# The 13 RMS norms of a two-block transformer kernel: squares taken from PSUM, sums on VectorE, root and reciprocal with tokens on partitions

## The reference, cut to what matters

```python
def rms_norm(x, w):
    xf = x.astype(jnp.float32)
    y = xf * lax.rsqrt(jnp.mean(xf * xf, axis=-1, keepdims=True) + EPS)
    return (y * w.astype(jnp.float32)).astype(x.dtype)
...
# first block, each layer (the ctx rows likewise in layer 0)
h_lat = rms_norm(x, norm_pre_mix[l]) * (1.0 + sc1) + sh1
x = x + g1 * rms_norm(y_lat, norm_post_mix[l])
h_lat = rms_norm(x, norm_pre_ffn[l]) * (1.0 + sc2) + sh2
x = x + g2 * rms_norm(conv_ffn(h_lat, ...), norm_post_ffn[l])
...
# second block, each layer, and at the end
x = x + token_mixing(x, mix_norm_g[l], ...)
h = rmsnorm(x, ffn_norm_g[l])
x = x + swiglu(h, ...)        # layer 0; a mixture of 8 experts in layer 1
return rmsnorm(x, final_norm_g)
```

## Time and profile before

| what | us |
|---|---|
| median of 3 runs | 3615.11 (3614.79 to 3618.42) |
| time of the profiled execution | 3617.53 |
| span of the profiled execution | 3615.8 |
| PE busy in it | 3414.6 |
| DVE busy | 793.5 |
| ACT busy | 670.2 |
| POOL busy | 129.4 |

### The profile page before, as it was taken

The page is one execution under the profiler, slowest core; times in us unless marked ns, Lnnn a source line. Parts: engine busy times, 40 slices in busy tenths (PEclk is TensorE's granted clock), DMA queues, the critical chain, the costliest instruction groups (busy, mean ns, idle before and its releaser), DMA issues.

```text
span 3615.8 us, 75672 instructions
## 1 busy us (share of the span) xinstructions
PE 3414.6 (94%) x32538; PEld 2801.5 (77%) x32539; DVE 793.5 (22%) x1762; ACT 670.2 (19%) x1444; POOL 129.4 (4%) x173
## 2 busy tenths in 40 slices
PE   7999689999989899999999999989999999999998
PEld 3456638884357688787788887779999999988898
DVE  1114626660111421113210023130000100011001
ACT  2224112220112431112210021201111111110011
POOL 0000010010000100010000010000000000000000
PEclk9999699999999999999999999989999999999999
DMA  6446011222223243343344433238999999954477
GB/s 247 183 164 225 11 47 70 93 70 72 78 82 103 90 151 130 115 146 110 116 140 144 158 128 105 100 111 320 358 350 370 372 354 352 370 188 154 136 267 272
DMA packets 94761, 637.59 MB, mean 176 GB/s; under 512 B 10784, under 2 KB 11824, under 8 KB 38592
## 3 DMA queue, kind: packets, MB, share of 16 engines
q1 hardware_dynamic: 92048, 627.58, 47.2%
q0 software_dynamic: 2608, 8.49, 0.7%
HBM read 634.98 MB, written 1.05 MB: 176 GB/s over the span
## 4 chain that ended last, share of the span: by engine, by line
PE 91%; DVE 4%; ACT 2%; DMA 2%; issue 1%; POOL 0%; SPq 0%; DVEq 0%; ACTq 0%
PE bank L504 23%; PE bank L924 20%; PE bank L594 18%; PE bank L545 7%; PE bank L614 5%; PE bank L516 4%; PE bank L881 2%; PE bank L468 2%; PE bank L478 1%; PE bank L650 1%; PE bank L939 1%; PE bank L632 1%; PE bank L639 1%; DVE RT L1437 1%; DVE Y L1454 1%
## 5 line engine op out<-in xcount | busy, mean ns | idle before, releaser
L504 PE MATMUL bank<-H,ring 128*128 128x256 f32 (+1 forms) x3040 | 774.1, 417 | 19.6 <-ACT H L1095 16.5
L504 PEld LDWEIGHTS bank<-H,ring 128*128 128x128 f32 x3040 | 581.2, 192 | 197.7 <-issue 127.2
L594 PE MATMUL bank<-PROJ,ring 128*64 128x96 f32 (+2 forms) x7776 | 668.0, 282 | 12.3 <-ACT SC L1136 9.6
L594 PEld LDWEIGHTS bank<-PROJ,ring 128*64 128x64 f32 (+1 forms) x7776 | 547.6, 147 | 131.3 <-issue 98.1
L924 PE MATMUL bank<-MIX,ring 128*64 128x96 f32 x12544 | 524.2, 247 | 10.8 <-issue 10.8
L924 PEld LDWEIGHTS bank<-MIX,ring 128*64 128x64 f32 x12544 | 522.4, 138 | 13.1 <-issue 12.9
L1821 DVE TENSOR_TENSOR PROJ<-SC,bank 128x96 f32 (+2 forms) x246 | 71.0, 288 | 626.1 <-ACT SC L1277 621.9
L924 PE MATMUL bank<-H,ring 128*128 128x256 f32 x896 | 193.7, 379 | 0.0
L924 PEld LDWEIGHTS bank<-H,ring 128*128 128x128 f32 x896 | 170.2, 190 | 23.4 <-issue 0.3
L614 PE MATMUL bank<-H,ring 128*128 128x256 f32 x768 | 178.6, 391 | 3.9 <-ACT PROJ L1158 3.7
L614 PEld LDWEIGHTS bank<-H,ring 128*128 128x128 f32 x768 | 148.5, 196 | 28.2 <-issue 7.4
(11 more groups left out here) (310 smaller groups left out, 2705.3 us busy)
## 6 DMA issues: line engine op xcount, KB each, us to landing
ring<-in_moe_up SPq DMA_DIRECT2D x224, 1024.0 KB, 6.0
ring<-in_moe_down SPq DMA_DIRECT2D x128, 896.0 KB, 6.0
ring<-in_up SPq DMA_DIRECT2D x44, 1024.0 KB, 4.8
ring<-in_mod_b SPq DMA_DIRECT2D x40, 1024.0 KB, 5.0
ring<-in_tproj SPq DMA_DIRECT2D x32, 1024.0 KB, 4.8
ring<-in_proj SPq DMA_DIRECT2D x26, 1024.0 KB, 4.8
ring<-in_gates SPq DMA_DIRECT2D x24, 1024.0 KB, 4.8
ring<-in_down SPq DMA_DIRECT2D x32, 704.0 KB, 4.1
```

Of the source, the lines that this page charges most:

```text
L504: mm = pe.matmul(B[(tile + t) % 4][:, 0:width], w[:, k, t * P:(t + 1) * P], src[:, k, 0:width], start=k == 0, stop=k == k_n - 1)
L594: mm = pe.matmul(B[bank][lo:lo + m, 0:width], w[:, k, lo:lo + m], src(s * half + k), start=s == 0 and k == 0, stop=s == 1 and k == half - 1)
```

## The change

- Post norms: ACT squares each tile from its PSUM bank into H and then copies it to Y with the factor AB as the copy's scale (`take_tile`). The tiles of an output projection are taken one by one, for which PE counts a new semaphore `half_unit` behind the first tile of each unit.
- DVE adds the squares of tiles 1 to 6 onto that of tile 0 (`sum_square`) for norms 0, 1, 3, 5, 7, 9, 10 and 11; PE then takes the means of two tiles (the sum, and tile 7). Norms 2, 4, 6, 8 and 12 keep a step for each of the 8 tiles.
- PE's means have the squared tile as weights and one column of constants as moving operand; tokens come out on partitions, in 4 columns of bank 7 (2 at width 256). ACT takes the root and DVE the reciprocal of these columns in `stat`, and PE spreads them into bank 4, which DVE's multiplies read.
- DVE multiplies a whole tile at once without the factor; in pre norms of the first block the factor is the scale of ACT's shift. DVE, not POOL, makes the residual adds.
- The square-root table of ACT is called up ahead of norms 0, 1, 3, 5, 7, 9, 10, 11 and 12 by a root of one column.

The diff, cut to its core:

```diff
+        HALF_OF = {"wout0": 0, "wout1": 4, "twout0": 8, "twout1": 12}
+        def tile_in(name, k):
+            if k % 2 == 0:
+                return S("half_unit"), HALF_OF[name] + k // 2 + 1
+            return unit_done, base[name] + k // 2 + 1
...
-            def norm(n, width):
-
-                for k in range(KT):
-                    pe.wait_ge(S(f"norm{n}_sq"), k + 1)
-                    mm = pe.matmul(B[4][:, 0:width], mean_d, H[:, k, 0:width], start=k == 0, stop=k == KT - 1)
-                mm.then_inc(S("norm_ms"), 1)
+            def norm(n, width, summed):
+
+                def means(k, first, last):
+                    for c in range(width // P):
+                        mm = pe.matmul(B[7][:, c:c + 1], H[:, k, c * P:(c + 1) * P], mean_d[:, 0:1], start=first and c == 0, stop=last,
+                                       skip_group_check=True)
+                    return mm
+
+                if summed:
+                    pe.wait_ge(S("norm_acc"), summed)
+                    means(0, True, False)
+                    pe.wait_ge(S(f"norm{n}_sq"), KT)
+                    means(KT - 1, False, True).then_inc(S("norm_ms"), 1)
+                else:
+                    for k in range(KT):
+                        pe.wait_ge(S(f"norm{n}_sq"), k + 1)
+                        mm = means(k, k == 0, k == KT - 1)
+                    mm.then_inc(S("norm_ms"), 1)
+                pe.wait_ge(S("norm_r"), n + 1)
+                for c in range(width // P):
+                    mm = pe.matmul(B[4][:, c * P:(c + 1) * P], stat[:, c:c + 1].to_broadcast([P, P]), ident, start=True, stop=True)
+                mm.then_inc(S("norm_b"), 1)
...
-                act.activation(RT[:, 0:width], B[4][:, 0:width], ACT.Sqrt, bias=eps).then_inc(S("norm_rt"), 1)
+                act.activation(stat[:, 0:width // P], B[7][:, 0:width // P], ACT.Sqrt, bias=eps).then_inc(S("norm_rt"), 1)
...
                 for k in range(KT):
+                    act.wait_ge(S(f"norm{n}_scaled"), k + 1)
                     for s in range(width // T):
-                        act.wait_ge(S(f"norm{n}_scaled"), k * (width // T) + s + 1)
                         part = H[:, k, s * T:(s + 1) * T]
-                        act.activation(part, part, ACT.Identity, bias=MOD[:, l, sh + k, s:s + 1]).then_inc(S(f"norm{n}_out"), 1)
+                        act.activation(part, part, ACT.Identity, bias=MOD[:, l, sh + k, s:s + 1], scale=AB[:, row, k, s:s + 1])\
+                           .then_inc(S(f"norm{n}_out"), 1)
...
+            def sqrt_table(src):
+                act.activation(qw[:, :], src, ACT.Sqrt)
+            def take_tile(n, k, bank, row, width):
+
+                act.activation(H[:, k, 0:width], bank[:, 0:width], ACT.Square).then_inc(S(f"norm{n}_sq"), 1)
+                for s in range(width // T):
+                    ins = act.activation(Y[:, k, s * T:(s + 1) * T], bank[:, s * T:(s + 1) * T], ACT.Copy, scale=AB[:, row, k, s:s + 1])
+                ins.then_inc(lin_free, 1)
...
+            def down_to_y(n, name, width):
+                sqrt_table(eps)
+                for k in range(KT):
+                    act.wait_ge(unit_done, base[name] + 2 * k + 2)
+                    take_tile(n, k, B[k % 2], 3, width)
...
+            def sum_square(n, k, width):
+
+                dve.wait_ge(S(f"norm{n}_sq"), k + 1)
+                ins = dve.tensor_tensor(H[:, 0, 0:width], H[:, 0, 0:width], H[:, k, 0:width], ALU.add)
+                if k < KT - 2:
+                    step(ins)
+                else:
+                    ins.then_inc(S("norm_acc"), 1)
+
             def recip_root(n, width):
                 dve.wait_ge(S("norm_rt"), n + 1)
-                step(dve.reciprocal(RT[:, 0:width], RT[:, 0:width]))
+                dve.reciprocal(stat[:, 0:width // P], stat[:, 0:width // P]).then_inc(S("norm_r"), 1)
+                dve.wait_ge(S("norm_b"), n + 1)
...
+                    dve.tensor_tensor(H[:, k, 0:width], X[:, k, 0:width], B[4][:, 0:width], ALU.mult).then_inc(S(f"norm{n}_scaled"), 1)
...
+            def residual(n, width):
+
+                for k in range(1, KT - 1):
+                    sum_square(n, k, width)
                 recip_root(n, width)
+                for k in range(KT + 1):
+                    if k < KT:
+                        dve.tensor_tensor(Y[:, k, 0:width], Y[:, k, 0:width], B[4][:, 0:width], ALU.mult).then_inc(S(f"norm{n}_scaled"), 1)
+                    if k > 0:
+                        dve.wait_ge(S(f"norm{n}_scaled"), k)
+                        dve.tensor_tensor(X[:, k - 1, 0:width], X[:, k - 1, 0:width], Y[:, k - 1, 0:width], ALU.add)\
+                           .then_inc(S(f"norm{n}_out"), 1)
...
-            residual(3, TC)
+            pool.wait_ge(S("norm_ms"), 4)
             for v in range(2, 2 * C_HEADS):
```

More of the change, by code:

```diff
@@ L493, in mod_step, with fm_unit @@
                     mod_turn(n - 1)
-            def fm_unit(u, tile, src, width, it=0, tiles_per_it=0, k_n=KT, ready=None, mod=None):
+            def fm_unit(u, tile, src, width, it=0, tiles_per_it=0, k_n=KT, ready=None, mod=None, half=False):
                 w = unit(u, it).rearrange("p (k n) -> p k n", n=2 * P)
@@ L505, in fm_unit @@
                                        start=k == 0, stop=k == k_n - 1)
+                    if t == 0 and half:
+                        mm.then_inc(S("half_unit"), 1)
                     if t == 0 and mod is not None:
@@ L521, in wout @@
                 for j in range(4):
-                    fm_unit(base[name] + j, tile_base[name] + 2 * j, src, width, ready=ready if j == 0 else None)
+                    fm_unit(base[name] + j, tile_base[name] + 2 * j, src, width, ready=ready if j == 0 else None, half=True)
             def pairs(name, width, ready):
@@ L1071, in _ @@
             moe()
-            norm(12, T)
+            norm(12, T, 0)
         @block.scalar
@@ L1439, in modulate @@
-            def modulate(n, row, width):
+                dve.reciprocal(stat[:, 0:width // P], stat[:, 0:width // P]).then_inc(S("norm_r"), 1)
+                dve.wait_ge(S("norm_b"), n + 1)
+            def modulate(n, width):
                 recip_root(n, width)
                 for k in range(KT):
-                    for s in range(width // T):
-                        cols = slice(s * T, (s + 1) * T)
-                        dve.scalar_tensor_tensor(out=H[:, k, cols], in0=X[:, k, cols], scalar=AB[:, row, k, s:s + 1],
-                                                 in1=RT[:, cols], op0=ALU.mult, op1=ALU.mult).then_inc(S(f"norm{n}_scaled"), 1)
@@ L1448, in gate @@
-            def gate(n, row, width):
-                recip_root(n, width)
-                for k in range(KT):
-                    for s in range(width // T):
-                        cols = slice(s * T, (s + 1) * T)
-                        dve.scalar_tensor_tensor(out=Y[:, k, cols], in0=Y[:, k, cols], scalar=AB[:, row, k, s:s + 1],
-                                                 in1=RT[:, cols], op0=ALU.mult, op1=ALU.mult).then_inc(S(f"norm{n}_scaled"), 1)
+                    dve.tensor_tensor(H[:, k, 0:width], X[:, k, 0:width], B[4][:, 0:width], ALU.mult).then_inc(S(f"norm{n}_scaled"), 1)
@@ L1863, in _ @@
             step(dve.tensor_copy(lmask[:, :], SC[:, 0:6 * 32]))
+            for k in range(1, KT - 1):
+                sum_square(0, k, TC)
             dve.wait_ge(S("consts_in"), 16)
@@ L1951, in _ @@
             step = Chain(pool, "pool_step")
-            def residual(n, width):
-                for k in range(KT):
-                    pool.wait_ge(S(f"norm{n}_scaled"), (k + 1) * (width // T))
-                    pool.tensor_tensor(X[:, k, 0:width], X[:, k, 0:width], Y[:, k, 0:width], ALU.add).then_inc(S(f"norm{n}_out"), 1)
             def conv_ffn(l, width):
```

100 lines of the change are left out of this document (49 added, 51 removed).

## The result

The changed kernel takes 3586.64 us (3582.56 to 3588.1, median of 4 runs) against 3614.95 for the kernel before on the same chip: ratio 0.9921, interval 0.9909 to 0.9933. That is 28.3 us less, where 46.4 were forecast, and 2.6 us above the upper end of the range. The profiled execution took 3587.29 us, its span is 3585.5, 30.3 us shorter than the span of before.

The account below looks back on a forecast made before the run. PE, busy 94% of the span, bounds the kernel, so only the norms' stretches can shorten. Savings of 11.7, 9.0, 5.2, 5.15, 7.2, 8.2 and 0 sum to 46.4 us: from 3615.1 to 3568.7 us, range 3551 to 3584.

Parts of the forecast that it names:

- the stretches: Nine windows from PE's last matmul before a norm or pair to its first behind it, together 154.7 us.
- Part 1: PE's end to post norm's first multiply: 4.1 us in place of 12.98 (width 512), 2.5 in place of 7.11 (256).
- Part 2: Post norm's first multiply to second norm's root: 16.6 us against 17.09 (width 512), 8.55 against 8.59 (256).
- Part 3: Second norm's root to PE's start: 4.6 us against 7.4 (width 512); 2.95 with a shift, 2.35 without (256).
- Rival B: Half clock lasts 4 to 6 us longer at each of 9 restarts behind the norms: 3591 us, chance 0.09.
- Rival A: PE's clock stays at 1.00 in the means, or loads don't follow it: 16.5 us more gained, 3552 us, chance 0.17.
- Rival C: Slower: each of nine restarts behind the norms runs 11 us longer at half clock; 3619 to 3625 us, chance 0.02.
- D: Change fails its aim: table load lands behind the means, or PE waits for DVE's sums; 3578 us, chance 0.05.

Follow-up runs that it names:

- experiment 3: The kernel before, with 96 harmless one-slot instructions added at the start of PE's program; 3623.77 us, ratio 1.0025.
- experiment 8: Against experiment 1: the pre-norms' factor back in DVE's multiplies, ACT's shift with its bias alone; 3560.7 us, ratio 0.9856.
- experiment 1: The changed kernel, with PE branching over the padding ahead of the experts' loop (max_nops=0); 3569.15 us, ratio 0.9872.
- experiment 2: The kernel before, with PE branching over the padding ahead of the experts' loop (max_nops=0); 3610.38 us, ratio 0.9984.
- experiment 9: Against experiment 1: DVE adds squares of tiles 0+1, 2+3, 4+5 in norms 2, 4, 6, 8 between residual adds; 3566.31 us, ratio 0.9867.
- 11, 12: Against experiment 1: DVE sums squares 4+5, 6+7 after its last residual add in norms 2, 4; 3561.07 us; with experiment 8's edit too, 3561.23 us.
- experiment 5: Against experiment 1: no sums of squares on DVE, PE takes the means of all 8 tiles in all 13 norms; 3601.89 us, ratio 0.9965.
- experiment 7: Against experiment 1: residual adds of norms 1, 3, 5, 7 back on POOL; 3567.12 us, ratio 0.9873.
- experiment 6: Against experiment 1: means by large matmuls, root and reciprocal on a tile as wide as the norm, no spread; 3574.58 us, ratio 0.9885.

## Why the prediction was wrong

**The chain and the stretches.** Forecast against measured, in us:

| stretch | before | forecast | after |
|---|---|---|---|
| norm 0 | 15.98 | 8.8, of it 0.7 behind it | 8.33 |
| (1, 2) | 37.47 | 25.8, of it 0.5 behind it | 24.55, and 1.30 behind it |
| (3, 4) | 35.17 | 26.2, of it 0.9 behind it | 24.68, and 1.29 behind it |
| (5, 6) | 19.17 | 14.0 | 13.40 |
| (7, 8) | 18.55 | 13.4 | 12.93 |
| 9, 10, 11 | 6.42, 6.33, 9.10 | 3.6, 3.6, 6.4 | 3.50, 3.40, 6.14 |
| 12 | 6.52 | 6.5 | 6.02 |

Each is within 0.6 us of the forecast (with what stands behind it counted), and the terms inside hold too. Part 1 of norm 1: 3.50 for 4.1, mostly since the spread ran at clock 1.00 (1.20 us from its start to the multiply, for which I took 1.7). Part 2 of norm 2: 16.45 for 16.6, PE's 64 pieces back to back. Part 3: 4.60 for 4.6. At width 256 the three parts behind wout1 took 2.38, 8.05 and 2.97 for 2.5, 8.55 and 2.95.

**The step that failed** is "Together 154.7 us, 4.3% of the span, are all that this change can shorten; layers between them keep their work." They keep their work, but the sentence looked only for what can shorten. The change also makes PE's program longer, by 78 float32 matmuls ahead of the experts' loop, and one line of the program puts in fillers whose number went by that length in all three traces that have them. The padding's cost was a term that the sum didn't have, taken at nothing without a reason. It grew from 26 to 226 recorded fillers, and a hole of 14.29 us opened in front of the experts' loop. Jumping over it gave 17.5 us in the changed kernel and 3.65 in the kernel before, so executed padding is 13.8 of the 18.1 us that the gain fell short. No rival had it: all four argued about the norms and what follows them. One row in the trace of before could have led to it: PE idle for 6.05 us ahead of L924 with the releaser "issue". It isn't the padding's own gap (experiment 3), but reading the code around it would have shown the line. The size is luck: 312 instructions more came out as 200 fillers more (512 - 312), and 96 more as 160 (256 - 96). With 262 more it would by the same count, an estimate from these traces, have been 6 fewer (256 - 262), 20 in place of the 26 that lay under matmuls in the kernel before, and no hole would have opened.

**A smaller term mis-sized: half clock behind the norms.** I charged 2.1 us for slower shifts and restarts. Up to the router the windows show 51.3 us saved and the pairing of matmuls a lead of 43.4, so the layers gave back 7.8. 2.6 are the first units behind norms 2 and 4, where ACT's shift paced at 7.97/16 = 0.50 us, not the 0.46 I took. The layers behind norms 8 and 10 gave back 2.5 and 5.3 (324.21 and 322.63 us before, both at a mean clock of 0.97; 326.73 and 327.92 after, at 0.96 and 0.95), and some others gained a little. Part of this can be seen in the small gates behind norm 10, before and after:

```profile
2080.65:2087.72 7.07, 7.07 (x33) 2.79 (x33) 2.71 (x7) 0.00 (x0) 0.00 (x0) 1.00 0.00 0
```

```profile
2034.90:2043.66 8.76, 8.76 (x33) 3.17 (x33) 2.69 (x7) 0.00 (x0) 0.00 (x0) 0.81 0.11 45
```

Same instructions, 1.69 us more at a mean clock of 0.81. In the profile of experiment 8 this very stretch took 7.1 again, and both layers their old times, so these pieces come and go from one kernel to the next; what decides it no run shows. Rival B had the kind right, but not the size: some 5 us, not 20 to 25. Better norms (3 us) and what the layers gave back beyond the 2.1 (6 us) partly cancel. That experiment 1 lands on the forecast to 0.4 us is in part chance: of its 44.9 us against the kernel before 3.65 come from the jump itself (experiment 2), and like with like the norms' change gives 41.2, 5 less than the 46.4 of the sum.

**Rival A** asked whether the means keep clock 1.00. They don't: 0.51 in part 2 of the pair (1, 2), with weight loads at 13.73/64 = 0.215 us. Nor do the loads stay as they were: at clock 1.00 the 8 spread pieces of norm 1 start 0.11 us apart, and at 0.50 a piece costs twice as much, with 1 moving column (0.213 us from start to start in norm 2) as with 128 (0.213 us in its spread). Rival C had no part in it, and of D neither half came: the roots and reciprocals took 0.26 and 0.18 us with no table load before them, and PE never waited for DVE's sums.

**Slips in the working** that changed no chance: 9 restarts of 4 to 6 us at half speed are 18 to 27 us (rival B says 20 to 25), and 9 x 11 / 2 is 49.5, not the 50 that rival C needs. And for norm 0 the mean clock of 0.93 was read as showing part of the stretch at half clock. That trace's clock record has no entry before 41.3 us, so its first 3.5 us count as 1.00 whatever they were; the choice to price norm 0 at half clock came out right (8.33 us).

## What to carry to other kernels

A change that adds or removes instructions moves everything behind them in that engine's program: before predicting, look for what depends on position (alignment, padding, a loop entry), and in the trace for idle time with the releaser "issue". Here executed padding was best jumped over or left out, and the alignment itself was worth nothing measurable. And where one engine paces a stretch, the pieces to save are those at its end: in norm 2 sums that PE had to wait for delayed its start by 6.18 us (experiment 9), while sums at the tail shortened the stretch (11, 12), until the next queue was in the way. The sums that gave the most (experiment 5) are those that DVE makes while PE is still busy with the layer before or, at norm 0, stands idle (1.95 us ahead of its first mean in the changed kernel).

## What the runs showed of the hardware that I had not expected

- Filler instructions in TensorE's program take time in bulk: 0.073 us each, with holes of 9.97 us at 186 recorded fillers and 14.29 us at 226.
- A matmul with one moving column goes by its weight load, and its pace follows the granted clock: 0.11 us from start to start at 1.00, 0.213 at 0.50. In pair (5, 6) of the changed kernel both paces stand in one run of pieces, on either side of the clock's fall at 1213.1 us: 0.11 within a tile's pieces up to 1213.24, 0.213 behind.
- Such pieces back to back didn't bring the clock back: 64 of them in norm 2 took 13.81 us at 0.50, and in norm 0 of experiment 5 64 took 13.78 us at the same pace.
- POOL's adds and DVE's instructions on two SBUF tiles slow each other (experiment 7): one of DVE's on 512 columns took 1.75 us beside the adds and 0.68 alone, and the squares that follow the adds started 1.67 us apart beside them and 1.24 apart while DVE read PSUM.
- A granted clock of 1.00 can mean that the record is empty. In norm 0 of the changed kernel the pieces took 0.213 us under "1.00", but that trace's clock record begins only at 49.1 us, with a rise to 1.00, and there the large matmuls behind the norm change too, from 0.85 us apart to 0.43:

```profile
46.77 0.34 PEld L528 LDWEIGHTS bank<-H,ring 128*128 128x128 f32 x1 [0.52 <-ACT H L1125]
...
48.48 0.34 PEld L528 LDWEIGHTS bank<-H,ring 128*128 128x128 f32 x1 [0.52 <-ACT H L1125]
...
49.67 0.19 PEld L528 LDWEIGHTS bank<-H,ring 128*128 128x128 f32 x1 [0.24 <-ACT H L1125]
```

In experiment 5, with 64 one-column pieces in norm 0, the record begins with a rise to 1.00 at 59.8 us; in the kernel before and in experiment 6, with large matmuls there, at 41.3 and 41.4. So norm 0 ran at half clock in the narrow form, and the load is no exception there.
